# A mixer and a top-4-of-32 expert layer on one core: all tokens are normalised and stored without the last expert, whose tokens are finished in slots behind its gate/up and scattered by an indirect DMA

## The reference

```python
x = _layer_norm(DEEPNORM_ALPHA * x + mixed, ln1_g[l], ln1_b[l])
ffn = _moe(x, ...)                       # 32 experts, each token goes to its top 4
x = _layer_norm(DEEPNORM_ALPHA * x + ffn, ln2_g[l], ln2_b[l])

# _moe, for the tokens xb of expert e:
h = xb @ w_gu[e] + b_gu[e]               # 1024 -> 2048
h_glu = jnp.minimum(h[:, :D_EXPERT], SWIGLU_LIMIT)
h_lin = jnp.clip(h[:, D_EXPERT:], -SWIGLU_LIMIT, SWIGLU_LIMIT)
act = h_glu * jax.nn.sigmoid(SWIGLU_ALPHA * h_glu) * (h_lin + 1.0)
y = act @ w_dn[e] + b_dn[e]              # 1024 -> 1024, summed with the token's gate
```

## Time and profile before

| | |
|---|---|
| median of 3 runs | 1030.18 us (1029.1 to 1030.41) |
| the profiled execution: time, span | 1029.9 us, 1028.2 us |
| moved by DMA in it | 422.64 MB, 411 GB/s over the span |
| PE, DVE, ACT, POOL busy | 831.2, 243.4, 73.1, 6.2 us |

### The profile page before, as it was taken

The page is one execution under the profiler, slowest core; times in us unless marked ns, Lnnn a source line. Parts: engine busy times, 40 slices in busy tenths (PEclk is TensorE's granted clock), DMA queues, the critical chain, the costliest instruction groups (busy, mean ns, idle before and its releaser), DMA issues.

```text
span 1028.2 us, 20061 instructions
## 1 busy us (share of the span) xinstructions
PE 831.2 (81%) x8403; PEld 359.9 (35%) x8404; DVE 243.4 (24%) x674; ACT 73.1 (7%) x173; POOL 6.2 (1%) x24
## 2 busy tenths in 40 slices
PE   9999879897659999986699977656966987876963
PEld 8885434333213334332233422222311322321321
DVE  2473712221112122211122211111201211211114
ACT  1030100000000000000000000000000000000000
POOL 1000000000000000000000000000000000000000
PEclk9999989999889999998899997898978899978988
DMA  9988699999999999999999999999999999999995
GB/s 333 413 334 327 267 426 424 428 428 428 429 428 429 428 429 428 428 428 428 429 425 428 428 428 428 428 428 430 429 428 428 428 428 428 428 428 428 428 426 214
DMA packets 38730, 422.64 MB, mean 411 GB/s; under 512 B 5884, under 2 KB 6328, under 8 KB 14264
## 3 DMA queue, kind: packets, MB, share of 16 engines
q1 hardware_dynamic: 36320, 421.93, 97.4%
q10 hardware_dynamic: 2392, 0.44, 0.2%
HBM read 421.31 MB, written 1.05 MB: 411 GB/s over the span
## 4 chain that ended last, share of the span: by engine, by line
DMA 51%; PE 40%; DVE 6%; issue 2%; DVEq 0%; ACT 0%; SPq 0%; POOL 0%; POOLq 0%
DMA dn_buf<-in_w_down_dram 51%; PE ps L885 14%; PE ps L918 13%; PE ps L722 5%; PE ps L765 3%; PE ps L879 2%; PE ps L739 1%; DVE act_t L677 1%; DVE lin L672 1%; DVE lin L675 1%; DVE glu L669 1%; DVE lin L670 1%; PE ps L714 0%; PE ps L798 0%; PE ps L753 0%
## 5 line engine op out<-in xcount | busy, mean ns | idle before, releaser
L885 PE MATMUL ps<-gu_buf,rows_t 128*32 128x512 f32 x2944 | 379.4, 661 | 112.6 <-DMA gu_buf<-in_w_gate_up_dram 112.6
L885 PEld LDWEIGHTS ps<-gu_buf,rows_t 128*32 128x32 f32 x2944 | 96.5, 116 | 383.4 <-issue 205.3
L918 PE MATMUL ps<-dn_buf,act_t 128*32 128x256 f32 x2912 | 175.0, 386 | 42.6 <-DMA dn_buf<-in_w_down_dram 34.3
L669 DVE TENSOR_SCALAR glu<-ps 128x256 f32<-128x256 f32 x46 | 19.5, 424 | 624.3 <-PE ps L885 624.3
L918 PEld LDWEIGHTS ps<-dn_buf,act_t 128*32 128x32 f32 x2912 | 90.2, 110 | 114.0 <-DMA dn_buf<-in_w_down_dram 46.0
L879 PE MATMUL ps<-turned,bias_sel 128*32 128x512 f32 x368 | 53.0, 649 | 25.0 <-issue 24.8
L407 ACT ACTIVATE sig<-glu 128x256 f32<-128x256 f32 x46 | 19.2, 417 | 560.9 <-DVE glu L669 560.9
L722 PE MATMUL ps<-turned,gu_buf 128*128 128x256 f32 x256 | 55.6, 379 | 0.0
L835 PE MATMUL ps<-xs,onehot 128*32 128x256 f32 x736 | 53.0, 409 | 1.4 <-DVE onehot L656 1.4
L859 PE MATMUL ps<-mix,back 32*128 32x256 f32 x736 | 53.7, 406 | 0.5 <-ACT mix L411 0.5
L722 PEld LDWEIGHTS ps<-turned,gu_buf 128*128 128x128 f32 x256 | 48.6, 190 | 6.6
(11 more groups left out here) (182 smaller groups left out, 263.8 us busy)
## 6 DMA issues: line engine op xcount, KB each, us to landing
gu_buf<-in_w_gate_up_dram SPq DMA_DIRECT2D x128, 2048.0 KB, 29.5
dn_buf<-in_w_down_dram SPq DMA_DIRECT2D x63, 2048.0 KB, 13.5
gu_buf<-in_w_in_dram SPq DMA_DIRECT2D x4, 2048.0 KB, 18.4
gu_buf<-in_w_out_dram SPq DMA_DIRECT2D x2, 2048.0 KB, 15.6
xs<-in_x_dram SPq DMA_DIRECT2D x2, 512.0 KB, 3.8
gu_buf<-in_w_in_dram SPq DMA_DIRECT2D x2, 512.0 KB, 6.8
gu_buf<-in_w_in_dram SPq DMA_DIRECT2D x1, 1024.0 KB, 9.4
late<-in_ln_g_dram SPq DMA_DIRECT2D x2, 512.0 KB, 20.1
```

What stands on the lines that cost most here:

```text
L669: V.tensor_scalar(glu[:], half(HB, 0), SWIGLU_LIMIT, None, ALU.min).then_inc(S["glu_ok"], 1)
L885: ins = T.matmul(ps[SLOTS * j:SLOTS * (j + 1), HB, :], rows_t[:, k, :], gu_buf[:, b, k, :].rearrange("p (two n) -> p two n", two=2)[:, :, ...
L918: ins = T.matmul(ps[SLOTS * j:SLOTS * (j + 1), YB, 0:QF], act_t[:, DK * m + q, :], weights[q][:, QF * j:QF * (j + 1)], start=(m == 0 and q ...
```

## The change

The last expert is taken out of the common sum. `last` is the number of blocks ahead of expert 31, and `past` is one more than the number of its own blocks; the loops over blocks on DVE and ACT now end at `last`. When expert 30 is in the sum, ACT copies the sum from PSUM to SBUF (`acc_sb`, in the half of `gu_buf` that no expert needs any more), PE spreads the gains and biases from one row by matmuls with a row of ones, and DVE normalises all 256 tokens into `settled`, which SP stores. This is the final result of every token that doesn't go to expert 31.

The tokens that do are finished in their slots by `final_block`. It is the block of before, with these differences: the gates come in with the activation; two small matmuls bring each slot's gate and token number (`slot_vals`); a one-hot product adds the token's row of `acc_sb` to the down product in the same PSUM bank; and the normalisation is done in the slot layout, where partition 32 j + s holds quarter j of slot s, so that PE combines the four quarters' statistics (`same_slot`). POOL then writes the 128 quarter rows of 1 KB over the rows in `out` by an indirect DMA, once the four stores have landed. Empty slots get a row number beyond the bounds and write nothing. The last 2 MB of down weights come as two transfers of 1 MB with a semaphore each, and the gains and biases are loaded as single rows ahead of SP's loop.

The core of the diff (8 columns of indent are cut; left out are the views in the spare half of `gu_buf`, the names of the semaphores, a longer `iota`, the gate/up part of `final_block`, which is that of before, and small operations):

```diff
+acc_sb = gu_buf[:, 0, 0, :].rearrange("p (h d) -> p h d", h=TH)
+settled = gu_buf[:, 0, 1, :].rearrange("p (h d) -> p h d", h=TH)
...
+    sp.dma_start(late[0:1, 0, :], ln2_g[0:1, :]).then_inc(S["ln2_in"], 16)
+    sp.dma_start(late[0:1, 1, :], ln2_b[0:1, :]).then_inc(S["ln2_in"], 16)
     with sp.Fori(2, E // 2) as pair:
         stream_dn(pair * 2 - 1)
         stream_gu(pair * 2, 0)
         stream_dn(pair * 2)
         stream_gu(pair * 2 + 1, 1)
-    stream_dn(E - 1)
-    sp.dma_start(late[:, 0, :], ln2_g[0:1, :].to_broadcast([P, D])).then_inc(S["ln2_in"], 16)
-    sp.dma_start(late[:, 1, :], ln2_b[0:1, :].to_broadcast([P, D])).then_inc(S["ln2_in"], 16)
+    last_used = blocks_before(E - 1)
+    stream_dn_chunk(E - 1, 0, last_used)
+    sp.wait_ge(dn_used[1], last_used)
+    for r, landed in ((DK, dn_in[1]), (DK + DK // 2, S["dn_last"])):
+        sp.dma_start(dn_buf[:, r:r + DK // 2, :].rearrange("p q n -> p (q n)"), dn_src[E - 1][:, D * r:D * (r + DK // 2)]).then_inc(landed, 16)
     for h in range(TH):
         for c in range(2):
             sp.wait_ge(S["fin_ok"], 2 * h + c + 1)
-            sp.dma_start(out_dst[:, h, 512 * c:512 * c + 512], xs[:, h, 512 * c:512 * c + 512]).then_inc(S["stored"], 16)
+            sp.dma_start(out_dst[:, h, 512 * c:512 * c + 512], settled[:, h, 512 * c:512 * c + 512]).then_inc(S["stored"], 16)
...
+    nc.gpsimd.memset(ones_row[:], 1.0).then_inc(S["ones_row"], 1)
...
+    past = pool.value_load(bounds[0:1, E + 1:E + 2], min_val=2, max_val=LASTB + 1)
+    with pool.Fori(1, past) as nth:
+        pool.wait_ge(S["z_var"], nth)
+        nc.gpsimd.tensor_tensor(z_rstd, z_var, small[:, 380:381], ALU.pow).then_inc(S["z_rstd"], 1)
+        pool.wait_ge(S["stored"], 16 * 2 * TH)
+        pool.wait_ge(S["z_ok"], nth)
+        nc.gpsimd.indirect_dma_start(out_rows, bass.IndirectOffsetOnAxis(ap=row_at, axis=0), z_row, None,
+                                     bounds_check=SEQ * GROUPS - 1, oob_is_err=False).then_inc(S["scattered"], 16)
...
-    n_blocks = act.value_load(bounds[0:1, E:E + 1], min_val=1, max_val=MAXB)
-    with act.Fori(0, n_blocks) as g:
+    last = act.value_load(bounds[0:1, E - 1:E], min_val=1, max_val=MAXB - 1)
+    with act.Fori(0, last) as g:
...
+    act.wait_ge(S["acc_done"], 1)
+    for j in range(GROUPS):
+        nc.scalar.copy(acc_sb[:, :, QF * j:QF * (j + 1)], ps[:, j, :].rearrange("p (h n) -> p h n", h=TH)).then_inc(S["acc_sb"], 1)
+    act.wait_ge(S["gq_ps"], 1)
+    nc.scalar.copy(slot_gb, ps[:, TB, :]).then_inc(S["gq_sb"], 1)
+    past = act.value_load(bounds[0:1, E + 1:E + 2], min_val=2, max_val=LASTB + 1)
+    with act.Fori(1, past) as nth:
+        act.wait_ge(S["glu_ok"], last + nth)
+        nc.scalar.activation(sig[:], glu[:], ACT.Sigmoid, scale=SWIGLU_ALPHA).then_inc(S["sig_ok"], 1)
...
+    V.tensor_scalar(bounds[0:1, E + 1:E + 2], nb[0:1, E - 1:E], 1.0, None, ALU.add)
...
-    dve.wait_ge(S["ln2_in"], 32)
     dve.wait_ge(S["acc_done"], 1)
...
+    V.tensor_copy(same_slot.rearrange("p (j e) -> p j e", j=GROUPS), stack_ident[:].unsqueeze(1).to_broadcast([P, GROUPS, E]))
...
+    for h in range(TH):
+        V.tensor_copy(tok_vals[:, h, 0:1], gates[:, h, E - 1:E])
+        ins = V.tensor_scalar(tok_vals[:, h, 1:2], part_iota[:], P * h + 1.0, None, ALU.add)
+    ins.then_inc(S["tok_vals"], 1)
+    for c in range(2):
+        dve.wait_ge(S["acc_sb"], 2 * c + 2)
+        for h in range(TH):
+            ins = V.bn_stats(stats[:, h, c, :], acc_sb[:, h, 512 * c:512 * c + 512])
+    link(ins)
+    for h in range(TH):
+        norm_variance(h, stats, S["fin_var"])
+    dve.wait_ge(S["gb_ps"], 1)
+    for h in range(TH):
+        for c in range(2):
+            V.scalar_tensor_tensor(settled[:, h, 512 * c:512 * c + 512], acc_sb[:, h, 512 * c:512 * c + 512], mv[:, h, 0:1],
+                                   ps[:, c, :], ALU.subtract, ALU.mult).then_inc(S["fin_centred"], 1)
+    for h in range(TH):
+        dve.wait_ge(S["fin_rstd"], h + 1)
+        for c in range(2):
+            dve.wait_ge(S["fin_centred"], 2 * h + c + 1)
+            v = settled[:, h, 512 * c:512 * c + 512]
+            V.scalar_tensor_tensor(v, v, small[:, 374 + h:375 + h], ps[:, 2 + c, :], ALU.mult, ALU.add).then_inc(S["fin_ok"], 1)
+    dve.wait_ge(S["gq_sb"], 1)
+    past = dve.value_load(bounds[0:1, E + 1:E + 2], min_val=2, max_val=LASTB + 1)
+    with dve.Fori(1, past) as nth:
+        now = last + nth
+        e_next = dve.value_load(expert_of[0:1, bass.ds(now, 1)], min_val=0, max_val=E - 1)
+        V.tensor_copy(gated[:], onehot[:].rearrange("p h j s -> p h (j s)")).then_inc(S["gated_ok"], 1)
+        dve.wait_ge(S["gated_ok"], now)
+        pick(block_base[:, bass.ds(now, 1)], lambda h: places[:, h, bass.ds(e_next, 1)]).then_inc(S["onehot_ok"], 1)
+        dve.wait_ge(S["h_ps"], now)
...
+        dve.wait_ge(S["slots_ps"], nth)
+        V.tensor_copy(slot_vals, ps[:, TB, 0:2]).then_inc(S["slot_sb"], 1)
+        dve.wait_ge(S["slot_sb"], nth)
+        dve.wait_ge(S["scaled_ok"], now)
+        dve.wait_ge(S["sig_ok"], now)
+        V.scalar_tensor_tensor(lin[:], lin[:], slot_vals[:, 0:1], sig[:], ALU.mult, ALU.mult).then_inc(S["act_ok"], 1)
+        dve.wait_ge(S["act_ok"], now)
+        V.transpose(act_t[:], in_blocks(lin[:])).then_inc(S["act_t_sb"], 1)
...
+        V.tensor_tensor(row_at, row_a, row_b, ALU.add)
...
+        dve.wait_ge(S["z_ps"], nth)
+        V.bn_stats(z_stats, half(YB, 0)).then_inc(S["z_parts"], 1)
+        dve.wait_ge(S["z_parts"], nth)
+        V.tensor_tensor(group_stats, z_stats.unsqueeze(1).to_broadcast([P, GROUPS, 6]),
+                        group_of.unsqueeze(2).to_broadcast([P, GROUPS, 6]), ALU.mult).then_inc(S["z_stats"], 1)
+        dve.wait_ge(S["gq_sb"], 1)
+        dve.wait_ge(S["stats_ps"], nth)
+        V.bn_aggr(z_mv, ps[:, TB, 64:88].rearrange("p (j s) -> p j s", j=GROUPS)).then_inc(S["z_mean"], 1)
+        dve.wait_ge(S["z_mean"], nth)
+        V.tensor_scalar(z_var, z_mv[:, 1:2], LN_EPS, None, ALU.add).then_inc(S["z_var"], 1)
+        V.scalar_tensor_tensor(z_mid, half(YB, 0), z_mv[:, 0:1], slot_gb[:, 0:QF], ALU.subtract, ALU.mult).then_inc(S["z_centred"], 1)
+        dve.wait_ge(S["z_centred"], nth)
+        dve.wait_ge(S["z_rstd"], nth)
+        V.scalar_tensor_tensor(z_row, z_mid, z_rstd, slot_gb[:, QF:2 * QF], ALU.mult, ALU.add).then_inc(S["z_ok"], 1)
+        dve.wait_ge(S["scattered"], nth * 16)
...
-    with pe.Fori(E // 2 - 1, E // 2) as pair:
-        pair_of_experts(pair)
-    n_blocks = pe.value_load(bounds[0:1, E:E + 1], min_val=1, max_val=MAXB)
-    pe.wait_ge(S["y_sb"], n_blocks)
-    pe.wait_ge(S["back_sb"], n_blocks)
+    e = E - 2
+    expert(e, 0, 16 * (E // 2), [down_at(0, e * 16), down_at(1, (e + 1) * 16)])
+    last = pe.value_load(bounds[0:1, E - 1:E], min_val=1, max_val=MAXB - 1)
+    pe.wait_ge(S["y_sb"], last)
+    pe.wait_ge(S["back_sb"], last)
     combine(0, back, y_sb)
     combine(1, back, y_sb).then_inc(S["acc_done"], 1)
+    pe.wait_ge(S["ln2_in"], 32)
+    pe.wait_ge(S["ones_row"], 1)
+    for n in range(2):
+        for j in range(GROUPS):
+            ins = T.matmul(ps[SLOTS * j:SLOTS * (j + 1), TB, QF * n:QF * (n + 1)], ones_row[:, 0:SLOTS], late[0:1, n, QF * j:QF * (j + 1)],
+                           start=True, stop=True, skip_group_check=True)
+    ins.then_inc(S["gq_ps"], 1)
+    pe.wait_ge(S["acc_sb"], GROUPS)
+    for n in range(2):
+        for c in range(2):
+            ins = T.matmul(ps[:, 2 * n + c, :], ones_row[:], late[0:1, n, 512 * c:512 * c + 512], start=True, stop=True)
+    ins.then_inc(S["gb_ps"], 1)
+    pe.wait_ge(S["tok_vals"], 1)
+    pe.wait_ge(S["gq_sb"], 1)
+    def final_block(now, nth):
...
+        ins.then_inc(S["h_ps"], 1)
+        pe.wait_ge(S["gated_ok"], now)
+        for h in range(TH):
+            ins = T.matmul(ps[:, TB, 0:2], gated[:, h, :], tok_vals[:, h, :], start=(h == 0), stop=(h == TH - 1))
+        ins.then_inc(S["slots_ps"], 1)
+        pe.wait_ge(S["onehot_ok"], now)
+        gather().then_inc(S["rows_ps"], 1)
+        for h in range(TH):
+            for j in range(GROUPS):
+                T.matmul(ps[SLOTS * j:SLOTS * (j + 1), YB, 0:QF], gated[:, h, 0:SLOTS], acc_sb[:, h, QF * j:QF * (j + 1)],
+                         start=(h == 0), stop=False)
+        pe.wait_ge(S["act_t_sb"], now)
+        for q in range(KT):
+            if q == 0:
+                pe.wait_ge(dn_in[0], 16 * (E - 1))
+            elif q == DK:
+                pe.wait_ge(dn_in[1], 16 * E)
+            elif q == DK + DK // 2:
+                pe.wait_ge(S["dn_last"], 16)
+            for j in range(GROUPS):
+                ins = T.matmul(ps[SLOTS * j:SLOTS * (j + 1), YB, 0:QF], act_t[:, q, :], dn_buf[:, q, QF * j:QF * (j + 1)],
+                               start=False, stop=(q == KT - 1))
+        ins.then_inc(S["z_ps"], 1)
+        pe.wait_ge(S["z_stats"], nth)
```

(41 more changed lines are left out.)

38 lines of the change are left out of this document (37 added, 1 removed).

## The result

The changed kernel took **1022.76 us** (median of 4 runs, 1022.2 to 1023.52) against 1029.99 of before: a ratio of 0.9925 with a 95% interval of 0.9912 to 0.9939, 7.2 us less, where 7.8 were forecast (1022.4). The profiled execution has a span of 1021.2 and took 1022.98.

A forecast was written before the change was run, and what follows sets the result against it. The tail behind the last weights' landing was taken as the bound: 0.1 + 3.83 + 3.5 = 7.43 against 15.27, so -7.8 us, 1022.1 for the profiled execution and 1022.4 for the median; range 1020.9 to 1026.

The forecast's parts named there:

- What bounds it: End of the kernel: DMA is busy until the last down weights land at 1012.93; only the 15.27 us behind that can pay.
- The start: One more tiny DVE operation before `bounds_ok`, for which SP waits with expert 2's weights: +0.1 us (bounds 0 and 0.2).
- The gap: Between 986 and 1012.93, where PE has little to do: the normalisation of 256 tokens moved there is covered, costing 0.
- the wide rows: PE's spreading of gains and biases by eight 128x512 matmuls before expert 31's block: 0.44 each, 3.5 us, done at 993.5.
- the fourth rival: Expert 31's block starts too late because PE's clock stays down from 993.5 over four chunks: +3.2, 1025.6; chance 0.04.
- Behind the landing: `final_block` from the last landing at 1012.93 through the last scaling to POOL: a sum of 3.83 us.
- the 24-column matmul: PE's matmul after the statistics, behind the last landing: 0.45 us to DVE's start, taken from the 32-column one.
- The first half of the step: PE behind the last landing: 8 matmuls in place of 16, 0.97, with hops 1.08 us.
- The scatter: POOL's indirect DMA, from `z_ok` to the end of the span: 2.52 as a plain store plus 1.0 for the list, 3.5.
- A one-off cost: First rival: POOL's first indirect DMA must fetch what it runs, 1.28 as ACT's table load, giving 1023.7; chance 0.13.
- A row: Second rival: POOL pays the scatter row by row; over 69 ns each nothing is gained, at 99 ns 1034.1; chance 0.07.
- The stores land in time: Denies the third rival: four stores share with the weights (2.45 later, 1024.9) or land after `z_ok` (1023.4); chance 0.10.

## Why the prediction was right

**What bounds it** held: the last landing stayed where it was (1012.88, again 1012.69), and 15.27 - 8.32 = 6.95 of the profiled gain of 7.0 stands behind it.

**The start**, reckoned at 0.1, cost nothing: from the transpose ahead of `bounds_ok` (L619, now L662) to SP's first issue of expert 2 it is 2.57 before and 2.56 after.

**The gap** had cover as forecast, with one term mis-sized: the wide rows of gains and biases took 4.85 (5.13 to 7.19 in the eleven other profiles of it and its versions) where the sum had 3.5. The sum went by rows at full clock. The windows of the changed kernel (granted clock third from the end) show it at 1.00 to 990 us and at 0.50 from 992 to 996, after PE had waited 1.18 for ACT's copies:

```profile
988.50:990.00 1.50, 1.50 (x4) 0.76 (x5) 1.50 (x3) 0.44 (x1) 0.00 (x0) 1.00 0.99 415
990.00:992.00 2.00, 2.00 (x5) 0.78 (x4) 0.76 (x5) 0.00 (x0) 1.07 (x2) 0.73 1.08 459
992.00:994.00 2.00, 2.00 (x6) 0.20 (x8) 0.61 (x1) 0.00 (x0) 0.00 (x0) 0.50 0.94 401
...
996.00:998.00 2.00, 2.00 (x16) 0.43 (x12) 2.00 (x4) 0.00 (x0) 0.00 (x0) 0.56 1.00 426
998.00:1000.00 2.00, 2.00 (x24) 0.60 (x20) 1.55 (x5) 0.00 (x0) 0.00 (x0) 1.00 1.04 442
```

This is the clock of the fourth rival, and what was said against it (PE is busy in just this stretch) didn't hold: the wide rows were slow in all twelve profiles. The rival's price didn't come, because the clock was back by 998, while it had reckoned four chunks at half clock. That the wide rows ended at 993.35 all the same, where the sum had 993.5, is luck: expert 30's product ended at 984.74 in this execution and not at 985.99. The slow rows cost nothing as long as PE still waits for a later chunk: in the version without the split, where they took 6.87, PE's wait for the fourth gate/up chunk was gone, but 2.2 of wait were left ahead of the last down chunk.

**Behind the landing** the sum had 3.83 to POOL's start on the scatter; the chain gives 4.33 (1012.88 to 1017.21). Of the 0.5, 0.27 are the 24-column matmul (0.72 with its hops where the row gave 0.45), again at half clock: it is 0.63 or 0.64 in the chains of four of the twelve profiles and 0.42 or less in the other eight. The first half of the step, 8 matmuls, is 1.18 and not 1.08, because a group of 16 rows doesn't take exactly half of 32 (1.07). The rest are hundredths in each hop.

**The scatter** had 3.5 (2.52 for a store and 1.0 for making the list) and took 4.04. The base was smaller (2.14 for a plain 128 KB store by SP) and the addition larger, 1.9: 1.1 for POOL's queue, which the sum hadn't as a term of its own, and 0.8 for the list. So the term came near by two errors that partly cancel, 0.4 too much and 0.9 too little; the 1.0 was a guess from POOL's one-column operations, and the split of the 1.9 was found only by the runs. The fit in the Trainium skill (DMA: Bandwidth & Descriptors, section "Anatomy of one DMA — SWDGE (gpsimd) path") gives an estimate of 2.3 us for this transfer. The trace has 2.6 from the instruction to the landing for the scatter and 2.2 for the plain store, which is near it; the 0.6 to 1.0 between the end of the scaling and the instruction and the 0.4 to 0.5 between the landing and the end of the span come on top.

**The rivals.** A one-off cost exists and is about 0.36, below the 1.28 taken from ACT's table load. The 6 us that the Trainium skill names (GPSIMD Engine Reference, section "Instruction dispatch") for a freshly loaded kernel don't appear in any run here. A row costs 4 ns and not 69. The stores land in time, and the weights don't wait for them.

**How near it came.** The two errors of half a microsecond each went the same way, and the missing cost at the start took 0.1 back, so the tail was 0.89 longer than forecast (8.32 against 7.43), which is also what the profiled execution is above its own forecast (1022.98 against 1022.1). That the median is only 0.36 above 1022.4 is luck: the profiled execution stood 0.3 under its median before and 0.2 above it after.

## What to carry to other kernels

Where a stream of weights sets the time, first read what stands behind its last landing, and move out of it whatever doesn't need the last bytes; here 256 tokens of normalisation and 1 MB of stores went into waits at no cost, and only the 32 slots of the last expert stayed. Then cut the last transfer, so that less work hangs on it, and look at the granted clock behind PE's waits: here it was halved after a wait of 1.2 us ahead of the wide rows in all twelve profiles and after one of 2.2 in the one without the split, and not after one of 2.9. An indirect DMA issued by POOL at the end of the chain is 1.9 us dearer than a plain store by SP; 0.36 of it went away when it wasn't the first, and 0.37 with three quarters of its rows, so most of it comes with every call, and the scatter pays only if it takes more than that out of the tail.
